# Moving the memory projections, sharing the first modulation sums between two engines, and splitting every weight slot on VectorE

## The reference

```python
mod = silu(c) @ ada_w + ada_b                      # c: one vector of 1024, ada_w: 1024 x 6144
shift1, scale1, gate1, shift2, scale2, gate2 = split(mod, 6)
u = rms_norm(x, norm1_g) * (1 + scale1) + shift1   # nothing of block 1 starts before this
z = u @ w_in                                       # q, k, v of two attentions, and their gates
y_a = nsa_attention(...) @ w_up_nsa
y_b = stick_breaking_attention(...) @ w_up_sb
x = x + gate1 * ((sigmoid(m_a) * y_a + sigmoid(m_b) * y_b) @ w_out)        # the first merging
x = x + gate2 * (square(relu(modulated_norm(x) @ mlp_w1)) @ mlp_w2)
# block 2
x = x + 0.5 * swiglu(rmsnorm(x, ffn1_norm), ffn1_w_gu, ffn1_w_down)
kv = rmsnorm(mem, mem_norm) @ mem_w_kv             # mem: 256 x 1024, an input of its own
k, v = rmsnorm(kv[:, :512] per head, k_norm), kv[:, 512:]   # first read late in block 2
x = x + merged(spatial gating, latent attention, memory attention(k, v)) @ w_out_2
x = x + 0.5 * swiglu(rmsnorm(x, ffn2_norm), ffn2_w_gu, ffn2_w_down)
```

## Time and profile before

| | |
|---|---|
| time, median of 3 runs | 1173.15 us (1172.92 to 1176.21) |
| the profiled execution | 1176.21 us, of it span 1174.5 us |
| granted TensorE clock, mean | 0.971 of 2.4 GHz |
| PE / DVE / ACT / POOL busy | 94% / 59% / 50% / 37% of the span |
| DMA, mean over the span | 174 GB/s |

### The profile page before, as it was taken

How to read it: one execution, slowest core, us unless ns; L and a number is a source line. 1 busy time by engine, 2 the same in 40 slices (tenths; PEclk the granted TensorE clock), 3 DMA queues, 4 the chain that set the end, 5 groups by cost and what they waited for, 6 DMA issues and landing times.

```text
span 1174.5 us, 21772 instructions
## 1 busy us (share of the span) xinstructions
PE 1106.4 (94%) x8468; PEld 1065.5 (91%) x8468; DVE 694.7 (59%) x1122; ACT 591.0 (50%) x1041; POOL 440.2 (37%) x236
## 2 busy tenths in 40 slices
PE   4789999899989999999999999999999887999999
PEld 3669999778889999999999998999899887999998
DVE  6545878887668843337777423665766774444421
ACT  4436565564455554444444445697544345444432
POOL 5440112112544544434444453323323244444442
PEclk8889999899989999999999999999899998999999
DMA  9546977213435555555555554444233343555553
GB/s 366 211 144 222 355 264 271 92 56 125 162 128 183 189 183 179 182 178 180 181 185 185 186 179 137 168 137 169 99 120 132 120 153 126 188 179 180 183 186 117
DMA packets 57651, 204.91 MB, mean 174 GB/s; under 512 B 6959, under 2 KB 8367, under 8 KB 57432
## 3 DMA queue, kind: packets, MB, share of 16 engines
q1 hardware_dynamic: 51176, 180.53, 45.0%
q0 software_dynamic: 6384, 23.09, 5.5%
HBM read 202.53 MB, written 1.06 MB: 173 GB/s over the span
## 4 chain that ended last, share of the span: by engine, by line
PE 79%; DVE 9%; DMA 4%; ACT 3%; issue 2%; POOL 1%; SPq 1%; DVEq 0%; ACTq 0%; POOLq 0%
PE bank L613 79%; DMA ring<-in_stream 2%; DMA ada_ring<-in_ada 2%; DVE ring_rounded L1610 1%; DVE ada_acc L1687 1%; PE bank L867 1%; ACT rounded_rounded L1215 1%; POOL ring_rounded L1140 1%; ACT wide L1397 1%; DVE wide L1858 1%; DVE shared L2125 1%; DVE wide_rounded L1887 0%; DVE shared_rounded L1887 0%; SPq L567 0%; DVE stats L1853 0%
## 5 line engine op out<-in xcount | busy, mean ns | idle before, releaser
L1140 POOL TENSOR_TENSOR ring_rounded<-ring,rounded_rounded 128x1024 fp32r<-128x1024 f32 x154 | 386.5, 2510 | 595.5 <-ACT rounded_rounded L1215 595.5
L613 PE MATMUL bank<-u_rounded,rounded_rounded 128*128 128x256 f32 x1528 | 442.9, 290 | 6.1 <-ACT u_rounded L1272 3.8
L613 PE MATMUL bank<-u_rounded,ring_rounded 128*128 128x256 f32 x1528 | 436.3, 286 | 0.0
L613 PE MATMUL bank<-u_lo_rounded,rounded_rounded 128*128 128x256 f32 x1528 | 430.8, 285 | 0.0
L1215 ACT ACTIVATE rounded_rounded<-ring 128x1024 fp32r<-128x1024 f32 x326 | 340.9, 1053 | 166.8 <-PE bank L613 146.5
L1610 DVE TENSOR_TENSOR ring_rounded<-ring,rounded_rounded 128x1024 fp32r<-128x1024 f32 x172 | 255.5, 1487 | 213.2 <-ACT rounded_rounded L1215 212.8
L613 PEld LDWEIGHTS bank<-u_rounded,rounded_rounded 128*128 128x128 f32 x1528 | 297.8, 195 | 10.9 <-issue 9.7
L613 PEld LDWEIGHTS bank<-u_rounded,ring_rounded 128*128 128x128 f32 x1528 | 297.7, 195 | 0.1
L613 PEld LDWEIGHTS bank<-u_lo_rounded,rounded_rounded 128*128 128x128 f32 x1528 | 294.1, 194 | 1.4 <-DVE u_lo_rounded L1656 0.4
L613 PE MATMUL bank<-shared_rounded,rounded_rounded 128*128 128x256 f32 x992 | 256.6, 286 | 2.8 <-DVE wide L1900 2.6
L613 PE MATMUL bank<-wide_rounded,rounded_rounded 128*128 128x256 f32 x864 | 234.7, 287 | 18.3 <-DVE shared_rounded L1887 5.7
(11 more groups left out here) (273 smaller groups left out, 1149.5 us busy)
## 6 DMA issues: line engine op xcount, KB each, us to landing
ring<-in_stream SPq DMA_DIRECT2D x328, 512.0 KB, 3.3
ada_ring<-in_ada POOLq DMA_DIRECT2D x33, 512.0 KB, 5.6
wide<-in_mem_t SPq DMA_DIRECT2D x2, 512.0 KB, 5.9
shared<-in_ada POOLq DMA_DIRECT2D x2, 512.0 KB, 10.0
ada_ring<-in_ada SPq DMA_DIRECT2D x2, 512.0 KB, 13.7
x<-in_x_t SPq DMA_DIRECT2D x1, 1024.0 KB, 14.1
wide<-in_ada POOLq DMA_DIRECT2D x2, 512.0 KB, 21.4
wide<-in_ada SPq DMA_DIRECT2D x2, 512.0 KB, 21.5
```

The source lines that it names most:

```text
L613: return nc.tensor.matmul(out, lhs, rhs, start=start, stop=stop, skip_group_check=True)
L1140: pool.tensor_tensor(R(w), w, R(slot_round(q)), ALU.subtract).then_inc(slot_split_by_pool, 1)
```

## The change

The chunks of `mem_w_kv_2` move in the stream: the keys' go behind `up_sb0`, `up_sb2`, `up_sb4`, `up_sb6`, the values' behind `mix7`. The memory is loaded after the first two parts of `ada_w` have been read, squared by ACT between the copies of `kc` and `vc`, its squares added up by POOL, its norm written by DVE behind `kb3`; both halves are stored to HBM and read back ahead of the first merging. Part 1 (scale1) is still summed by DVE; part 0 (shift1) by TensorE, with silu(c)[k] spread over 128 columns as stationary operand. POOL splits no slot. POOL adds up five blocks of squares instead of seven for two of the four norms, and in the two SwiGLUs the sum comes behind the first projection.

```diff
-ADA_ARRIVAL = (1, 3, 5, 7, 9, 0, 11, 13, 2, 15, 4, 6, 8, 10, 12, 14)
-EARLY_SLOTS = 10
+ADA_BEFORE_MEM, ADA_OVER_MEM = 21, 29
+ADA_BY_POOL_QUEUE = ((0, 0), (1, 0), (1, 1), (0, 2), (0, 3), (1, 5), (0, 4), (0, 5), (0, 7))
+ADA_BY_SP_QUEUE = ((0, 1), (1, 2), (1, 3), (1, 4), (1, 6), (1, 7), (0, 6))
...
         def by_pool(q):
-            return q < EARLY_SLOTS or (q % 2 == 1 and q >= first_of_pool)
+            return False
+        def gathered_blocks(row):
+            return KD - 3 if row in (ROW_1, ROW_3) else KD - 1
...
# SP
+            for half, name in ((slice(0, 4), "x"), (slice(4, 8), "x_end")):
+                sp.dma_start(x[:, half, :], x_t[:, half, :]).then_inc(loaded[name], 16)
+            for part_and_chunk in ADA_BY_SP_QUEUE[:4]:
+                load_ada_early(*part_and_chunk)
+            sp.dma_start(mats[:, MAT["ident"], :], mats_d[:, MAT["ident"], :]).then_inc(ident_loaded, 16)
             load(0, 0)
+            for part_and_chunk in ADA_BY_SP_QUEUE[4:]:
+                load_ada_early(*part_and_chunk)
...
+            full(sp, "ada0b")
+            for half, name in ((slice(0, 4), "mem"), (slice(4, 8), "mem_end")):
+                sp.dma_start(mem_n[:, half, :], mem_t[:, half, :]).then_inc(loaded[name], 16)
# TensorE
+            def shift_block(k):
+                pe.wait_ge(ada_early_full[0, k], 16)
+                for half, c in enumerate("ab"):
+                    name = f"ada0{c}"
+                    ps = bank(name) if k else claim(name)
+                    ins = mm(ps[:, :], c_spread[:, k, :], ada_early[0, k][:, half * 512:(half + 1) * 512], k == 0, k == KD - 1)
+                    if k == KD - 1:
+                        done(ins, name)
+            shift_block(0)
             sum_row("x_ss", ROW_X, merged)
+            for k in range(1, 5):
+                shift_block(k)
+            pe.wait_ge(scale_summed, KD)
+            done(ada_columns(claim("ada1"), 1, 0), "ada1")
+            for k in range(5, KD):
+                shift_block(k)
+            project_tokens(["vsw0", "vsw1"], KD, u_parts, 256, ready=lambda i: pe.wait_ge(u_ready, ROW_X * KD + i + 1))
...
             for m in range(KD):
                 project(f"up_nsa{m}", ...)
+                if m % 2:
+                    sum_squares(f"mem_k{m // 2}", "ones")
                 project(f"up_sb{m}", ...)
+                if m == 0:
+                    pe.wait_ge(loaded["mem_back"], 32)
+                if m % 2 == 0:
+                    project(f"mem_k{m // 2}", KD, mem_parts)
             for m in range(KD):
                 project(f"mix{m}", ...)
-            sum_gathered("x1_ss", ROW_1)
+            project_tokens(["mem_v0", "mem_v1"], KD, mem_parts, 512, lambda: sum_gathered("x1_ss", ROW_1))
             project_first("w1_0", u_parts, ROW_1)
...
             def swiglu(p, row, before):
                 project_first(f"{p}g0", u_parts, row)
+                sum_gathered(f"x{row - ROW_1 + 1}_ss", row)
# POOL
-            for q in range(EARLY_SLOTS - 2):
-                split_slot(q)
+            pool.wait_ge(row_squares_ready, (ROW_MEM + 1) * KD)
+            for n in (4, 2, 1):
+                ins = pool.tensor_tensor(mem_squares[:, 0:n, :], mem_squares[:, 0:n, :], mem_squares[:, n:2 * n, :], ALU.add)
+            for n in range(ADA_BEFORE_MEM, ADA_OVER_MEM):
+                load_ada(n)
+            pool.wait_ge(u_rounded, (ROW_MEM + 1) * KD)
+            pool.dma_start(mem_parts_kept[0], R(mem_n)).then_inc(mem_stored, 16)
+            pool.wait_ge(u_ready, (ROW_MEM + 1) * KD)
+            pool.dma_start(mem_parts_kept[1], R(mem_n_lo)).then_inc(mem_stored, 16)
+            for n in range(ADA_OVER_MEM, 48):
+                load_ada(n)
# DVE
+            v.tensor_scalar(c_spread, c_act[:, 1, :].unsqueeze(2).to_broadcast([P, KD, P]), 0.5, None, ALU.mult)
+            for k in range(KD):          # scale1 alone: 8 steps in place of 16
+                v.scalar_tensor_tensor(out=acc, in0=ada_early[1, k], scalar=c, in1=acc, op0=ALU.mult, op1=ALU.add)
+            def shift_diagonal(half):    # the diagonal of each 128x128 of the spread sum
+                v.tensor_tensor(kept, bank(name)..., mat("ident").unsqueeze(1).to_broadcast([P, 4, P]), ALU.mult)
+                v.tensor_reduce(out=mod[:, 4 * half:4 * half + 4], in_=kept, axis=AX.X, op=ALU.add)
...
             for b in range(4):
                 ahead(f"kb{b}")
                 ada_step()
+            norm_row(mem_n, mem_n_lo, mem_n, gains("mem_norm_2"), ROW_MEM, None, lambda: ahead("qb0"))
             for b in range(3):
                 ahead(f"qb{b}")
                 ada_step()
```

More of the change, by code:

```diff
@@ L105, in stream_chunks @@
     half = [span(k * P) for k in range(4)]
-    for b in range(4):
-        stationary("mem_w_kv_2", span(b * P), full)
-    moving("mem_w_kv_2", 512, 512, KD)
     for k in range(KD):
@@ L262, in proj_names @@
 def proj_names():
[L263 to L266 removed]
+    out = ["x_ss"]
+    out += ["vsw0", "vsw1", "vsb0", "vsb1", "ga", "bias", "kc", "vc", "ks", "kw"]
+    out += [f"qa{b}" for b in range(4)] + ["kb0", "kb1", "mem_ss", "kb2", "kb3"] + [f"qb{b}" for b in range(4)]
     out += ["ada2", "cmp_hid_k", "cmp_hid_v", "ada3", "ma0", "cmp_turn_k", "cmp_turn_v"]
@@ L751, in _ @@
[L751 to L760 removed]
+            u_parts, hidden_parts, mem_parts = (u, u_lo), (hidden, hidden_lo), (mem_hi, mem_lo)
@@ L1649, in norm_row @@
                 if meanwhile:
-                    ahead(meanwhile, 0)
+                    meanwhile()
                 for i in range(KD):
@@ new lines, in _ @@
+            scale = mod[:, 8:16]
+            full(dve, "ada1")
+            ins = v.scalar_tensor_tensor(out=scale, in0=bank("ada1")[:, 0:KD], scalar=1.0, in1=ada_bias(1), op0=ALU.add, op1=ALU.add)
+            free(ins, "ada1")
+            evacuated(dve, "ada1")
+            step(v.tensor_tensor(scale, scale, gains("norm1_g"), ALU.mult))
+            dve.wait_ge(row_rinv_ready, ROW_X + 1)
+            for i in range(KD):
+                v.scalar_tensor_tensor(out=u_lo[:, i, :], in0=x[:, i, :], scalar=mod[:, 8 + i:9 + i], in1=row_rinv[:, :],
+                                       op0=ALU.mult, op1=ALU.mult).then_inc(u_normed, 1)
@@ new lines, in shift_half @@
+            def shift_half(half):
+                shift_diagonal(half)
+                at = slice(4 * half, 4 * half + 4)
+                v.tensor_tensor(mod[:, at], mod[:, at], ada_bias(0)[:, at], ALU.add).then_inc(shift_ready, 1)
+                dve.wait_ge(shift_ready, half + 1)
+            shift_half(0)
+            for i in range(KD):
+                if i == 2:
+                    shift_half(1)
+                if i == 4:
+                    ahead("x_ss", 2)
+                dve.wait_ge(u_rounded, ROW_X * KD + i + 1)
+                v.scalar_tensor_tensor(out=R(u_lo[:, i, :]), in0=u_lo[:, i, :], scalar=mod[:, i:i + 1], in1=R(u[:, i, :]),
+                                       op0=ALU.add, op1=ALU.subtract).then_inc(u_ready, 1)
@@ L1740, in _ @@
+            output("bias")
+            free(v.tensor_copy(bias_line, bank("bias")[0:8, :]), "bias")
             dve.wait_ge(zeros_ready, 4)
```

277 lines of the change are left out of this document (144 added, 133 removed).

## The result

The changed kernel takes 1163.43 us (median of 4 runs, 1159.3 to 1164.07) beside 1173.77 for the kernel before in the same runs: a ratio of 0.9903, 95% interval 0.9883 to 0.9924. It is faster, by 10.3 us and not by 24.

What follows compares the result with a forecast made beforehand. TensorE, busy 94% of the span, was taken as the bound. Terms -39.4 + 24.6 - 4 - 4.5 - 3.6 - 4 + 6 + 1 = -23.9 us took the median from 1173.15 to 1149, range 1137 to 1165.

Steps and rivals of the forecast that it cites:

- joint with the other `ada_w` parts: Behind `kb3`, the memory's norm on DVE delays sums 11 to 16 and TensorE's fourth sum: +6 us, bounds 0 to +14.
- Start, -39.4: u's first matmul at 40.2 us instead of 79.93; u's projections run as if begun at 40.5: -39.4 us, bounds -44 to -32.
- The rival of the low clock: Shift blocks at the start stay at 1.2 GHz, sum at 43 us, `vsw` loses 2 more: +7, 1156 us; chance 0.12.
- +1 for the squares: ACT's squares of the memory between `kc` and `vc`, against four rounded slots in hand: +1 us, bounds 0 to 3.
- Memory's products +24.6: Memory's keys 11.5, values 10.8 and five fp32 sums 2.3 us come back in full TensorE time: +24.6 us.
- merging -4: First merging: TensorE's 3.9 idle us are filled by 24 more matmuls for every two m: -4 us.
- norm before `w1_0` -4.5: The memory's values now lie over the norm where TensorE stood still: -4.5 us, bounds -7 to -1.
- Splits on DVE alone, -4: Without POOL's splits blocking DVE, the 5.7 us of waits on subtractions in the mergings should mostly go: -4 us.
- Sums behind the first product -3.6: Sums of squares behind the first projection, POOL without splits: -3 us before `f2g0`, -0.6 before `f1g0`.
- the joints don't close: Rival: merging, norm and sums stay chains of ACT and DVE, giving none of 4 + 4.5 + 3.6 + 4: 1165 us; chance 0.15.
- My own test: Forecast wrong if u starts after 46 us, or TensorE's waits on L1610 in the second block exceed 10 us in sum.
- the 5 to 8 that I had listed as confirming: Sign listed for the forecast: TensorE waits 5 to 8 us before the fourth sum of `ada_w`.

Runs made afterwards that it cites:

- pool_splits: Changed kernel with GpSimd taking back every second split from the gates' second half on, all else as changed: 1178.61 us, ratio 1.0032 to the kernel before.

## Why the prediction was wrong, by its own steps

The direction was right; of the 24 us the medians show 10.3 and the traces 13.4. The step that failed is the joint with the other `ada_w` parts, the second point below. By the table of events the sum of -23.9 and the measured -13.4 part at these steps:

- **Start, -39.4: measured -35.4.** u's first matmul is at 42.67, not 40.2, and `vsw` runs behind DVE for some matmuls more. Two things: the scale's last chunk let DVE begin its last step only at 28.75 (I had the sum ready at 26), and TensorE then ran its columns and the next block at half pace:

```profile
30.09 3.57 PE L632 MATMUL bank<-half_column,ada_acc 128*128 128x1 f32 x16 [4.65 <-DVE ada_acc L1783]
33.53 3.59 PE L632 MATMUL bank<-mem_v,u 128*128 128x512 f32 x4
36.95 1.88 PE L632 MATMUL bank<-wide,u 128*128 128x512 f32 x4
```

  A block of 3.59 us and one of 1.88 are the two clock levels (1.2 and 2.4 GHz; granted 0.50 from 30.0 to 36.8 us, 1.00 before it), behind a wait of 4.65. The columns and that block cost 1.7 us each by it. The forecast had that much in it: all at full clock was 34, and I took 38. What it lacked is the wait for the scale's sum; the last block ended at 40.6. And `vsw` took 8.0 us in place of 6.2, with a clock granted at 0.50 from 43.7 to 47.0, behind a wait of 2.12 for the first u. The rival of the low clock, which I had given 0.12, had the last block at 43 and 2 us more in `vsw`: of its 7 us some 4 came, and half of them by a wait and not by the clock. By the Trainium skill (TensorE: Matmul & The Clock Gate, "HAM oscillation — how this bites in real kernels") bursts between transfer waits each run low. Here it was so behind the wait of 4.65 us, whose last cause was a chunk. It was not so behind that of 1.83 us for a chunk at 23.46: its block took 1.98 us, at a granted clock of 1.00.
- **Joint with the other `ada_w` parts, +6, and +1 for the squares: measured +16.2.** This is the step that failed. I had its queue (norm and rest on DVE, with a wait for ACT in the middle, steps 11 to 16 and the fourth sum behind) but counted DVE's work of 6.5 us, not what stands still while the engines wait for each other. ACT waiting for DVE's norm rounds no slot, so TensorE lost 4.67 us on a weight, which I hadn't thought of. DVE, behind the norm, freed no place for the next chunks, so TensorE waited another 6.07 before the fourth sum. Around both waits the clock was low, for 3.4 and 10.2 us, by an estimate from these lengths and TensorE's busy time in them 4 us more lost than before. The upper bounds of the two terms, 14 and 3, just hold it; the 7 that I took doesn't come to half. Left out, the norm gives 15 us; 40 us earlier, 12 of them.
- **Memory's products +24.6, merging -4, norm before `w1_0` -4.5: together +16.1, measured +15.0.** Right, part by part, though the splits' edit has a share in it that the sum had elsewhere (`pool_splits` took 5 us longer in these stages). Keys with merging cost 8.6 between the merging's start and its first addition to x (to 308.6 before, to 291.9 after; I had 11.5 and some sums, less 4), values and norm the other 6.4 (I had 10.8 less 4.5). A slip in the sum: five products at half of 1.02 us are 2.6, not 2.3.
- **Splits on DVE alone, -4: right in kind, wrong in place and size.** The wait of 5.7 in the mergings, which I had read as its price, is 5.8 after: it has another cause. The gain came in the attention: -6.1 us, where I had put nothing, and -7.0 with this edit alone. In the kernel before the merging takes it back. Undone in the changed kernel the edit costs 15 us, alone in the kernel before it gives none, so as a term of a sum it had no size.
- **Sums behind the first product -3.6, with the -4 above: -7.6 from w2 on, measured -3.1.** TensorE still waits 4.3 us for the rounded u in the second SwiGLU; the sum was ahead of it before, ACT's rounding is now. The stage from there to the first block of output is 138.3 us, 0.5 shorter than before. A wait of 3.96 us for a split at 804.9 is new, and one of 2.23 at 832.4 is gone.

In sum: 4.0 short at the start, 9.2 in the joint, 4.5 late, and 6.1 and 1.1 the other way: 10.5, which is 23.9 less 13.4. Of the rivals "the joints don't close" (1165) has the number but not the mechanism: merging and norm did close, and it was a new joint that opened; that the time came so near to it is chance. My own test, u's start after 46 us or over 10 us of waits on the splits in the second block, was met by neither. The wait before the fourth sum came out at 6.07, within the 5 to 8 that I had listed as confirming, while the term that it stood for was less than half of what was measured: I had not listed the split's wait ahead of it, nor the clock around both.

## What to carry to other kernels

Price a step that is moved by who stands still for it and not by its busy time: for each engine, write down what is queued behind each wait of the moved step, the rounding of the next weights and the issuing of later loads included, and look for a stretch in which these queues are empty; here the same work cost 15 us in one place and 2 to 4 us in another 40 us earlier. To price one edit out of several, undo it in the new kernel and also make it alone in the old one, and compare stage by stage: here one gave 15 us and the other nothing, and the stages showed a gain of 5 to 7 us in the attention in both, lost again in the merging of one, and in the other 7 us that came only from undoing it. And before comparing two layouts of the same work, see that the pitch of the saturated stage is the same in both: an unused tile was worth more here than the whole change.

## What the runs showed of the hardware that I had not expected

- 32 or 64 bytes of shift of x, u and the tiles behind them made a saturated stage 2 to 3% faster at full clock: 0.1167 or 0.118 us a 256-column matmul in place of 0.1200. 32 bytes took 18 us off 1174 and 23 off 1163, 64 bytes 16 off 1163. Why is open.
- POOL's three sums over 4, 2 and 1 blocks of squares took 6.38 us, and a step of DVE that met them 2.90 in place of 1.28.
- Beside GpSimd's splits, DVE's operations on six elements took 2.15 us where they met one (three of eight) and 0.16 where they didn't. The price of sharing fell on the smallest operations of the chain.
- In the second SwiGLU of `pool_splits` every block had such a meeting (2.16 us in place of 0.42) and TensorE's pace followed, 6.16 us a block in place of 5.76; in the first SwiGLU, with the same operations, none had.
